# The residual's first load over two queues, and no products of ones between the rows' transpose and the residual's, in a one-core Trainium2 layer stack

## The chip, the cores and the metric

The kernel runs on one core of a Trainium2 chip. A core has a matrix engine (TensorE, PE in the profile, PEld for its weight loads), a vector engine (VectorE, DVE), an activation engine (ScalarE, ACT), GpSimd (POOL) and SyncE (SP), which here only issues transfers. Each engine works through its own instructions in order and waits on semaphores for the others. Transfers between device memory and the core's memory (SBUF, 128 partitions) are issued by SyncE or ScalarE, each on a queue of its own, and run on 16 DMA engines.

The metric is the device time of one execution in microseconds; lower is better.

## What is computed

Three layers over one sequence of 256 tokens with 1024 features, in float32: two of a first kind (a mixer, then a squared-ReLU MLP) and one of a second kind (attention and a short convolution beside each other). Cut to the frame, and to what the kernel's first microseconds compute:

```python
def rmsnorm(x, g):
    xf = x.astype(jnp.float32)
    y = xf * lax.rsqrt(jnp.mean(xf * xf, axis=-1, keepdims=True) + EPS)
    return (y * g.astype(jnp.float32)).astype(x.dtype)

for l in range(DEPTH):                       # DEPTH = 2
    g = norm_g[l]
    h = rmsnorm(x, g[0])
    y = even_mixer(h, ...) if l % 2 == 0 else odd_mixer(h, ...)
    x = x + rmsnorm(y, g[1])
    h = rmsnorm(x, g[2])
    x = x + rmsnorm(sq_relu_mlp(h, mlp_w1[l], mlp_w2[l]), g[3])
# then one hybrid layer (attention, gated convolution) and a last rmsnorm
```

The even mixer begins with `p = (h @ w_in)`; its first columns to be computed are those of `hf` (512 to 1024).

## The kernel before

**The weights come in units.** All weight matrices are cut into 1 MB units, in a fixed order (`UNITS`). SyncE loads unit after unit into a ring of four slots `raw`; ScalarE casts each to its high half `wh`, VectorE subtracts to get the low half `wl` (a *split*), and TensorE multiplies high and low halves of weights and activations: three products in place of one in float32. Of the activations, `hh` and `hl` (tile `hx` in the rows) are the high and low half. Unit 0 is loaded, cast and split in two halves.

**The start.** Nothing can be multiplied before the first normalised residual stands transposed in `hx`. The steps, in order of what feeds what:

- SyncE loads the residual `x` in two transfers of 128 tokens (128 partitions, 4 KB in each; semaphores `d_x0` and `d_x1`), then the two halves of unit 0, then units 1 and 2, then small tables.
- ScalarE first issues two transfers on its own queue: `ident`, the identity matrix for transposes (64 KB), and `rows1`, 121 rows of gains and small parameters (60.5 KB; tile `arena` in the rows); both count on `d_rows`. Then it loads a function table and takes a root of `eps`, and for each 128 tokens takes the sum of squares (waiting for `d_x0`, `d_x1`) and a root.
- VectorE (`prenorm_first`) takes the reciprocal and scales the first 128 tokens into `work_t` (semaphore `x_w`). Then it waits for `colsT`, copies the transposed rows out of their bank into `col1` (`cols`), and then does reciprocal and scaling of the second 128 tokens.
- TensorE multiplies ones by ones eight times (`idle_products(8)`, a result that nobody reads), waits for `d_rows`, transposes the rows (`colsT`), makes three more such products, and then in `x_turn_first` waits for `x_w` and transposes 2 x 8 blocks of the residual: the eight of the first tokens, then the eight of the second, signalling `x_t` after every second block of these.
- ScalarE, after the cast of unit 0's first half, waits for `x_t` and multiplies each transposed block pair by its gain into `hh`; VectorE makes `hl`; and TensorE starts unit 0 (`a_first`).

The order on each engine is the order in the code; no scheduler moves anything. The helper at L672 issues all matrix products, L1843 ScalarE's activations, L1230 to L1236 VectorE's operations. In the trace one float32 product or transpose is one or two records: the eight products of ones are 16, the 16 transposes of the residual are 16.

Of the kernel before, what the change touches and what calls it, by code (L numbers as in the profile page):

```python
# [24 lines left out]
P = 128  # L25
# [201 lines left out]
def at(role, i=0):  # L227

    return next(u for u, it in enumerate(UNITS) if it[4] == role and it[5] == i)
# [39 lines left out]
def build(nc, a, out):  # L269
    ctx = ExitStack()  # L270
    with ctx:
# [3 lines left out]
        def place(name, shape, dt, at_byte=None):  # L275
            size = int(np.prod(shape[1:])) * (1 if dt == U8 else 4)
            if at_byte is None:
                at_byte = cursor[0]
                cursor[0] += (size + 31) // 32 * 32
            return nc.alloc_sbuf_tensor_at(name, list(shape), dt, offset=at_byte)  # L280
# [4 lines left out]
        x = place("x", (P, TT, D), F32)  # L285
# [60 lines left out]
        S = {n: ctx.enter_context(nc.semaphore("s_" + n)) for n in names}  # L346
# [132 lines left out]
        def half_of(half):  # L479
            return slice(512 * half, 512 * (half + 1))  # L480
# [12 lines left out]
        def turn_count(p, j):  # L493
            return {0: 0, 2: len(TURNS[0])}[p] + j + 1
# [44 lines left out]
        def wait_low(eng, u):  # L539

            eng.wait_ge(S["lo_" + LOW_OF[u][0]], LOW_OF[u][1])

        def unit_src(u):
            kind, w, r0, c0, _, _ = UNITS[u]
            n, cols = P * SLABS[kind], UELEMS // SLABS[kind]
            return a[w][r0:r0 + n, c0:c0 + cols].rearrange("(k p) c -> p k c", p=P)
# [9 lines left out]
        def slot(t, u):  # L556
            return part(t, u).rearrange("p (k c) -> p k c", k=SLABS[UNITS[u][0]])
# [44 lines left out]

        @block.sync
        def _(eng):
            eng.dma_start(x[:, 0, :], a["x"][0:P, :]).then_inc(S["d_x0"], 16)
            eng.dma_start(x[:, 1, :], a["x"][P:2 * P, :]).then_inc(S["d_x1"], 16)
            for u in range(NU):
                if u == 3:
                    eng.dma_start(rows2[0:ROWS2, :], a["rows2"]).then_inc(S["d_small"], 16)
                    eng.dma_start(rel_in, a["rel_bias"]).then_inc(S["d_small"], 16)  # L610
                    eng.dma_start(onehot, a["tbl"][0:32, T_ONEHOT:T_ONEHOT + SEQ]).then_inc(S["d_small"], 16)
                if u == 6:
                    eng.dma_start(mask_rows, a["tbl"][:, T_MASKS:T_END]).then_inc(S["d_masks"], 16)
                if u == RING:
                    eng.dma_start(tables[:, :], a["tbl"][:, 0:T_CAUSAL]).then_inc(S["d_tables"], 16)
                if u == 8:
                    eng.dma_start(wg[:, :, :],
                                  a["od_w_in"][:, 3072:3080].rearrange("(k p) c -> p k c", p=P)).then_inc(S["d_wg"], 16)
                    eng.dma_start(gzb[:, :], a["gate_b"].broadcast_to([P, 8])).then_inc(S["d_wg"], 16)
                if u == at("mv"):  # L620

                    eng.wait_ge(S["y_ret"], 2)
                    eng.dma_start(tables[:, 0:384], a["tbl"][:, T_CAUSAL:T_CAUSAL + 384]).then_inc(S["d_causal"], 16)
                for n, (v, i) in enumerate((("up0", 3), ("up0", 8), ("up1", 3), ("up1", 8))):
                    if u == at(v, i):
                        if n % 2 == 0:
                            eng.wait_ge(S["yl_turn"], turn_count(n, len(TURNS[n]) - 1))
                        else:
                            eng.wait_ge(S["x_n"], 4 * n)
                        src = a["rows1"]  # L630
                        eng.dma_start(grow, bass.AP(tensor=src.tensor, offset=src.offset + P * (16 * n + 8),
                                                    ap=[[0, P], [1, D]])).then_inc(S["d_grow"], 16)
                if u == at("aq", 1):
                    eng.wait_ge(S["mod"], 12)
                    eng.dma_start(gate_dram.rearrange("o (k p) -> p (o k)", p=P), mod[:, 16:24],
                                  allow_slow_non_contiguous=True).then_inc(S["d_gate"], 16)
                if u == at("out5"):

                    eng.wait_ge(S["aout"], ATT_HEADS)
                    eng.wait_ge(S["d_gate"], 16)  # L640
                    eng.dma_start(fin_gate, gate_dram.broadcast_to([P, D])).then_inc(S["d_gain"], 16)
                    eng.dma_start(fin_gain, a["final_gain"].broadcast_to([P, D])).then_inc(S["d_gain"], 16)
                if u == at("av"):

                    eng.wait_ge(S["warg"], HEADS)
                    eng.wait_ge(S["gbm"], 1)
                    eng.wait_ge(S["d_u"], 16)
                    src = scratch_dram
                    eng.dma_start(bias[:, :, :], bass.AP(tensor=src.tensor, offset=src.offset,
                                                         ap=[[1, P], [384, ATT_HEADS], [1, SEQ]])).then_inc(S["d_bias"], 16)  # L650
                if u >= RING:

                    wait_low(eng, u - RING)
                if u == 0:
                    for half, landed in enumerate((S["raw_half"], raw_sem[0])):
                        c = slice(4 * half, 4 * half + 4)
                        eng.dma_start(slot(raw, 0)[:, c, :], unit_src(0)[:, c, :]).then_inc(landed, 16)
                else:
                    eng.dma_start(slot(raw, u), unit_src(u)).then_inc(raw_sem[u % RING], 16)

            for t in range(TT):
                for half, done in enumerate((S["fin_act"], S["fin_dve"])):
                    if (t, half) != (1, 0):
                        eng.wait_ge(done, t + 1)
                        eng.dma_start(out[t * P:(t + 1) * P, half_of(half)], fin_t[:, t, half_of(half)]).then_inc(S["d_out"], 16)
            eng.wait_ge(S["d_out"], 64)
# [3 lines left out]
        def _(eng):  # L670
            def mm(o, l, r, start, stop):
                return eng.matmul(o, l, r, start=start, stop=stop, skip_group_check=True)  # L672
# [267 lines left out]
            def x_turn_first():  # L940

                for t in range(TT):
                    eng.wait_ge(S["x_w"], t + 1)
                    for k in range(KT):
                        m = eng.transpose(x_bank(k)[:, t * P:(t + 1) * P], work_t[:, t, k * P:(k + 1) * P], ident[:, :])  # L945
                        if t == 1 and k % 2 == 1:
                            m.then_inc(S["x_t"], 1)

            def idle_products(n):

                for _ in range(n):
                    mm(PS[1][:, 0:SEQ], ones[:, 0:1].broadcast_to([P, P]), ones[:, 0:1].broadcast_to([P, SEQ]), True, True)
# [2 lines left out]
            idle_products(8)  # L955
            eng.wait_ge(S["d_rows"], 32)
            eng.transpose(PS[2][:, 0:ROWS1], rows1[0:ROWS1, :], ident[0:ROWS1, 0:ROWS1]).then_inc(S["colsT"], 1)
            idle_products(3)
            x_turn_first()
            eng.wait_ge(S["const"], 2)  # L960

# [879 lines left out]
        def _(eng):  # L1841
            def act(o, x, f, **more):
                return eng.activation(o, x, f, **more)  # L1843
# [13 lines left out]
            def x_root(n, t):  # L1857

                squares(junk_x[:, t, :], x[:, t, :], 4 + t, S["x_ssq"])
                eng.wait_ge(S["x_ssq"], 2 * n + t + 1)  # L1860
                root(sd[:, t:t + 1], st[:, 4 + t:5 + t], D).then_inc(S["x_sd"], 1)
# [18 lines left out]

            def prenorm_first():
                for t in range(TT):
                    eng.wait_ge((S["d_x0"], S["d_x1"])[t], 16)
                    x_root(0, t)
                high_half(0)
                eng.wait_ge(S["cols"], 1)
                for k in range(KT):
                    if k == 4:
                        high_half(1)
                    if k % 2 == 0:  # L1890
                        eng.wait_ge(S["x_t"], k // 2 + 1)
                    act(hh[:, k, :], x_bank(k), ACT.Copy, scale=col1[:, R_NORM + k:R_NORM + k + 1]).then_inc(S["hh"], 1)
                high(1)
# [74 lines left out]
            def load_roots():  # L1968

                act(sd[:, 15:16], eps[:, :], ACT.Sqrt)  # L1970

            eng.dma_start(ident[:, :], a["tbl"][:, T_IDENT:T_IDENT + P]).then_inc(S["d_rows"], 16)
            eng.dma_start(rows1[0:ROWS1, :], a["rows1"]).then_inc(S["d_rows"], 16)
            eng.wait_ge(S["const"], 2)
# [147 lines left out]
            for u in range(-AHEAD, NU):  # L2122
# [53 lines left out]
                elif role in ("rq", "rk"):  # L2176
# [4 lines left out]
                    half = P // 2  # L2181
# [110 lines left out]
```

## Time and profile before

| | |
|---|---|
| median of 3 runs | 973.98 us (973.92 to 974.48) |
| the profiled execution's own time | 974.07 us |
| its span, first to last instruction | 972.0 us |
| TensorE busy | 964.2 us (99%) |
| VectorE busy | 682.1 us (70%) |
| ScalarE busy | 539.9 us (56%) |
| TensorE's first product of unit 0 | 10.80 us after the span's start |

The shares are averages over the span. The change touches only the first eleven microseconds, so the timeline and the chain of waits of that stretch are the views to read; the share of busy time says only that TensorE has hardly a gap after them. A busy TensorE at the start includes the products of ones, which compute nothing. A row of the timeline gives start, duration, engine, line and tiles, and in brackets how long the engine sat idle before and what ended that.

### The profile page before, as it was taken

What the parts mean: (1) busy time and instruction counts of PE and PEld (TensorE: products, weight loads), DVE (VectorE), ACT (ScalarE), POOL (GpSimd) and SP (SyncE); (2) the same over time, 40 slices, a digit from 0 to 9 for tenths busy, and PEclk for the clock granted to TensorE, in tenths of its full rate; (3) what the DMA queues carried; (4) which work ended last, traced back from release to release, by engine and by line L of the source; (5) the groups of instructions that cost most, each with busy time, mean ns of one, the idle gap of its engine ahead of it and who ended that gap; (6) DMA issues with size and microseconds to landing.
All of it is one profiled execution on the core that took longest, in us unless ns stands there. A gap on an engine that the chain in (4) does not pass through costs nothing.

```text
span 972.0 us, 13041 instructions
## 1 busy us (share of the span) xinstructions
PE 964.2 (99%) x5192; PEld 832.9 (86%) x5192; DVE 682.1 (70%) x917; ACT 539.9 (56%) x733; POOL 13.9 (1%) x12
## 2 busy tenths in 40 slices
PE   9999999999999999999999999999999999999997
PEld 8898888888888888988888888887888888888886
DVE  6989646687677767866687767768554888756474
ACT  7844464664555457655674455558445576545533
POOL 0000000000000000000000000000000000002000
PEclk9999999999999999999999999999999999999999
DMA  9954526467776674534467777773855544566611
GB/s 330 302 174 130 173 89 197 130 228 265 226 242 225 231 245 135 178 130 130 152 216 256 242 225 243 247 219 117 271 194 178 170 139 165 173 215 221 207 51 43
DMA packets 122863, 187.27 MB, mean 193 GB/s; under 512 B 5331, under 2 KB 88756, under 8 KB 122804
## 3 DMA queue, kind: packets, MB, share of 16 engines
q1 hardware_dynamic: 122368, 186.05, 58.1%
q8 instruction: 41, 0.67, 0.3%
q10 hardware_dynamic: 436, 0.40, 0.1%
q14 instruction: 18, 0.15, 0.0%
HBM read 185.37 MB, written 1.06 MB: 192 GB/s over the span
## 4 chain that ended last, share of the span: by engine, by line
PE 96%; DVE 3%; ACT 1%; issue 0%; ACTq 0%
PE bank L672 94%; DVE arena L1236 1%; DVE wl L1230 1%; PE bank L936 1%; PE bank L1026 0%; ACT arena L1843 0%; DVE arena L1233 0%; DVE arena L1230 0%; PE bank L1109 0%; ACT L1843 0%; ACT wh L1848 0%; PE bank L879 0%; PE bank L735 0%; PE bank L945 0%; ACT sd L1843 0%
## 5 line engine op out<-in xcount | busy, mean ns | idle before, releaser
L1230 DVE TENSOR_TENSOR wl<-raw,wh 128x2048 fp32r<-128x2048 f32 (+1 forms) x157 | 356.7, 2275 | 152.1 <-ACT wh L1848 128.1
L1848 ACT CAST wh<-raw 128x2048 fp32r<-128x2048 f32 x155 | 294.7, 1911 | 142.7 <-PE bank L672 141.0
L672 PE MATMUL bank<-hx,wh 128*128 128x512 f32 (+1 forms) x1280 | 296.6, 364 | 0.1
L672 PEld LDWEIGHTS bank<-hx,wh 128*128 128x128 f32 x1280 | 219.4, 190 | 30.4 <-issue 0.7
L672 PE MATMUL bank<-wh,hx 128*128 128x512 f32 x576 | 184.5, 394 | 0.8 <-ACT hx L1843 0.5
L672 PE MATMUL bank<-hx,wl 128*128 128x256 f32 x1088 | 174.3, 282 | 0.0
L672 PEld LDWEIGHTS bank<-hx,wl 128*128 128x128 f32 x1088 | 156.7, 190 | 8.9
L672 PE MATMUL bank<-wh,yh 128*128 128x512 f32 (+1 forms) x420 | 163.4, 389 | 0.0
L672 PE MATMUL bank<-wl,yh 128*128 128x512 f32 (+1 forms) x420 | 162.7, 387 | 0.0
L672 PE MATMUL bank<-wh,yl 128*128 128x512 f32 (+1 forms) x420 | 162.6, 387 | 0.0
L672 PEld LDWEIGHTS bank<-wh,hx 128*128 128x128 f32 x576 | 107.8, 188 | 24.3 <-issue 2.0
L672 PE MATMUL bank<-wl,hx 128*128 128x512 f32 x288 | 112.2, 390 | 0.0
L672 PEld LDWEIGHTS bank<-wh,yl 128*128 128x128 f32 x420 | 78.9, 188 | 16.2
L672 PEld LDWEIGHTS bank<-wh,yh 128*128 128x128 f32 x420 | 78.9, 188 | 15.5
L672 PEld LDWEIGHTS bank<-wl,yh 128*128 128x128 f32 x420 | 79.0, 188 | 15.3
L1230 DVE TENSOR_TENSOR arena<-bank,arena 128x256 f32<-128x256 f32 (+1 forms) x89 | 40.7, 488 | 44.3 <-ACT arena L2195 29.5
L672 PEld LDWEIGHTS bank<-wl,hx 128*128 128x128 f32 x288 | 54.1, 188 | 10.6
L2195 ACT COPY arena<-bank 128x256 f32<-128x256 f32 x56 | 18.1, 376 | 74.1 <-PE bank L672 74.1
L1988 ACT COPY work<-bank 128x256 f32<-128x256 f32 x56 | 20.6, 368 | 52.2 <-PE bank L672 52.2
L1843 ACT ACTIVATE arena<-bank 128x512 f32<-128x512 f32 (+2 forms) x58 | 28.4, 498 | 32.9 <-PE bank L672 32.8
L1236 DVE SCALAR_TENSOR_TENSOR arena<-raw,cf,arena 128x256 f32<-128x256 f32 x84 | 40.7, 485 | 3.0
L1843 ACT ACT_TABLE_LOAD x26 | 33.4, 1283 | 4.3 <-PE bank L672 2.0
(187 smaller groups left out, 675.0 us busy)
## 6 DMA issues: line engine op xcount, KB each, us to landing
raw<-in_mlp_w SPq DMA_DIRECT2D x64, 1024.0 KB, 5.4
raw<-in_w_in SPq DMA_DIRECT2D x40, 1024.0 KB, 5.1
raw<-in_ev_w_in SPq DMA_DIRECT2D x19, 1024.0 KB, 5.5
raw<-in_w_ada SPq DMA_DIRECT2D x12, 1024.0 KB, 5.1
raw<-in_od_w_in SPq DMA_DIRECT2D x12, 1024.0 KB, 5.2
raw<-in_ev_w_out SPq DMA_DIRECT2D x6, 1024.0 KB, 4.9
raw<-in_od_w_out SPq DMA_DIRECT2D x4, 1024.0 KB, 4.8
raw<-in_w_o_conv SPq DMA_DIRECT2D x4, 1024.0 KB, 4.8
```

Of the source, the lines that this page charges most:

```text
L672: return eng.matmul(o, l, r, start=start, stop=stop, skip_group_check=True)
L936: m = eng.transpose(x_half(t, k), src[:, t, k * P:(k + 1) * P], ident[:, :])
L1230: return eng.tensor_tensor(o, x, y, op)
L1236: return eng.scalar_tensor_tensor(out=o, in0=x, scalar=c, in1=y, op0=op0, op1=op1)
L1843: return eng.activation(o, x, f, **more)
L1848: eng.copy(part(wh, u), part(raw, u)).then_inc(S["hi"], 1)
L1988: eng.copy(up_home(i)[:, g * SEQ:(g + 1) * SEQ], up_block(u, g)[1][:, SEQ:2 * SEQ]).then_inc(S["up_low"], 1)
L2195: m = eng.copy(wide_home(u, g), wide_bank(u, g)[:, SEQ:2 * SEQ])
```

## The change

Two edits. First, each transfer of `x` is cut into two of 64 partitions: SyncE issues the lower halves, ScalarE the upper ones, both counting on the semaphore of their 128 tokens, for which ScalarE's squares now wait for 32. ScalarE issues its two before `ident` and `rows1`, so that these come third and fourth in its queue. Second, `idle_products(3)` between the transpose of the rows and that of the residual is gone; the eight before stay.

```diff
         @block.sync
         def _(eng):
-            eng.dma_start(x[:, 0, :], a["x"][0:P, :]).then_inc(S["d_x0"], 16)
-            eng.dma_start(x[:, 1, :], a["x"][P:2 * P, :]).then_inc(S["d_x1"], 16)
+            half = P // 2
+            eng.dma_start(x[0:half, 0, :], a["x"][0:half, :]).then_inc(S["d_x0"], 16)
+            eng.dma_start(x[0:half, 1, :], a["x"][P:P + half, :]).then_inc(S["d_x1"], 16)
...
             eng.transpose(PS[2][:, 0:ROWS1], rows1[0:ROWS1, :], ident[0:ROWS1, 0:ROWS1]).then_inc(S["colsT"], 1)
-            idle_products(3)
             x_turn_first()
...
                 for t in range(TT):
-                    eng.wait_ge((S["d_x0"], S["d_x1"])[t], 16)
+                    eng.wait_ge((S["d_x0"], S["d_x1"])[t], 32)
                     x_root(0, t)
...
+            half = P // 2
+            eng.dma_start(x[half:P, 0, :], a["x"][half:P, :]).then_inc(S["d_x0"], 16)
+            eng.dma_start(x[half:P, 1, :], a["x"][P + half:2 * P, :]).then_inc(S["d_x1"], 16)
             eng.dma_start(ident[:, :], a["tbl"][:, T_IDENT:T_IDENT + P]).then_inc(S["d_rows"], 16)
             eng.dma_start(rows1[0:ROWS1, :], a["rows1"]).then_inc(S["d_rows"], 16)
```

TensorE's instructions at the program's start, in the kernel before (`bank` is the destination; `ones` the products of ones, `ident,arena` the rows' transpose, `ident,work` the residual's, `hx,wh` unit 0):

```order
1 L672 MATMUL bank<-ones 128x256 x8
2 L957 MATMUL bank<-ident,arena 128x121
3 L672 MATMUL bank<-ones 128x256 x3
4 L945 MATMUL bank<-ident,work 128x128 x16
5 L672 MATMUL bank<-hx,wh 128x256 x8
```

and in the changed kernel:

```order
1 L673 MATMUL bank<-ones 128x256 x8
2 L958 MATMUL bank<-ident,arena 128x121
3 L946 MATMUL bank<-ident,work 128x128 x16
4 L673 MATMUL bank<-hx,wh 128x256 x8
5 L673 MATMUL bank<-hx,wl 128x256 x8
```

The residual's transposes now stand directly behind the rows'. ScalarE's instructions at the program's start, as the difference from the kernel before (line numbers shift by one to three):

```order
-L1972 DMA ident<-in_tbl 128x128
-L1973 DMA arena<-in_rows 121x128
+L1973 DMA x<-in_x 64x1024
+L1974 DMA x<-in_x 64x1024
+L1975 DMA ident<-in_tbl 128x128
+L1976 DMA arena<-in_rows 121x128
 L1843 ACT_TABLE_LOAD
 L1843 ACTIVATE sd<-eps 128x1
```

Two transfers have come ahead of the two that were there, and ahead of the table load; VectorE's instructions are unchanged.

## Rows read from the trace of the kernel before

**Rows 1.** The page: busy time, share of the span, instructions; shares of the chain.
```profile
PE 964.2 (99%) x5192; PEld 832.9 (86%) x5192; DVE 682.1 (70%) x917; ACT 539.9 (56%) x733; POOL 13.9 (1%) x12
...
PE 96%; DVE 3%; ACT 1%; issue 0%; ACTq 0%
```

**Rows 2.** The chain in order of time, start us, us, what; 0 to 31 us.
```profile
0.92 6.65 PE bank L672 x16
...
7.68 1.31 PE bank L672 x6
8.99 1.75 PE bank L945 x16
...
10.80 17.82 PE bank L672 x144
```

**Rows 3.** The timeline, 0 to 30 us: start us, us, engine, line; idle before.
```profile
0.74 0.42 ACTq L1972 DMA_DIRECT2D ident<-in_tbl  x1
...
1.19 0.63 ACTq L1973 DMA_DIRECT2D arena<-in_rows  x1
...
1.86 1.28 ACT L1843 ACT_TABLE_LOAD   x1 [1.86 <-issue]
...
4.87 1.06 ACT L1843 ACTIVATE arena<-x 128x1024 f32<-128x1024 f32 x1 [1.52 <-DMA x<-in_x]
...
6.26 1.04 ACT L1843 ACTIVATE arena<-x 128x1024 f32<-128x1024 f32 x1
...
6.66 0.75 DVE L1233 TENSOR_SCALAR work<-x,rs 128x1024 f32<-128x1024 f32 x1
...
7.42 0.29 ACT L1843 ACTIVATE sd<-st,eps 128x1 f32<-128x1 f32 x1
...
7.72 0.28 DVE L1281 COPY col<-bank 128x121 f32<-128x121 f32 x1 [0.31 <-PE bank L957]
...
8.11 0.75 DVE L1233 TENSOR_SCALAR work<-x,rs 128x1024 f32<-128x1024 f32 x1
8.41 1.05 ACT L1879 CAST wh<-raw 128x1024 fp32r<-128x1024 f32 x1 [0.70 <-DMA raw<-in_ev_w_in]
...
8.83 1.91 PE L945 MATMUL bank<-ident,work 128*128 128x128 f32 x16
9.56 1.22 DVE L1230 TENSOR_TENSOR wl<-raw,wh 128x1024 fp32r<-128x1024 f32 x1 [0.70 <-ACT wh L1879]
...
10.19 1.57 ACT L1843 ACTIVATE hx<-bank,col 128x256 fp32r<-128x256 f32 x4 [0.72 <-PE bank L945]
...
11.06 1.66 DVE L1236 SCALAR_TENSOR_TENSOR hx<-bank,col,hx 128x256 fp32r<-128x256 f32 x4 [0.27 <-ACT hx L1843]
...
16.12 4.48 DVE L1230 TENSOR_TENSOR wl<-raw,wh 128x2048 fp32r<-128x2048 f32 x2
...
22.70 0.40 PE L672 MATMUL bank<-hx,wh 128*128 128x256 f32 x2
```

**Rows 4.** Windows: us, busy us by engine (x), PEclk, DMA busy share, GB/s.
```profile
1.00:2.00 1.00, 1.00 (x3) 0.82 (x4) 0.31 (x1) 0.14 (x1) 0.00 (x0) 1.00 0.36 61
2.00:3.00 1.00, 1.00 (x4) 0.81 (x3) 0.00 (x0) 1.00 (x1) 0.00 (x0) 1.00 0.63 200
3.00:4.00 1.00, 1.00 (x3) 0.79 (x3) 0.00 (x0) 0.34 (x2) 0.00 (x0) 1.00 1.00 366
4.00:5.00 1.00, 1.00 (x4) 0.74 (x3) 0.00 (x0) 0.13 (x1) 0.00 (x0) 1.00 1.06 417
```

**Rows 5.** The tile x, 0 to 12 us, SyncE's two loads.
```profile
DMA to landing us min/median/max: 4.1/4.6/5.0
```

**Rows 6.** Products of ones, by form: 0.9 to 6.9 us, then 6.9 to 8.6.
```profile
L672 PE MATMUL bank<-ones 128*128 128x256 f32 x14 | 6.2, 634 | 0.9 <-DVE eps L1353 0.9
...
L672 PE MATMUL bank<-ones 128*128 128x256 f32 x8 | 2.1, 396 | 0.0
```

**Rows 7.** TensorE's longest wait behind the start: us in total, times, longest us.
```profile
PE bank L672 <- ACT hx L1843: 0.5, 1, 0.5
```

## The prediction, made before the changed kernel ran

> **What bounds the kernel now.** Begin with the page: TensorE is busy for 99% of the span, and the chain that ended last is 96% TensorE [rows 1]. Moving the start of the first real product moves the end, unless a later stage waits for something that doesn't move along. The list of TensorE's waits has little in it; the longest after the start is 0.5 us [rows 7]. So two questions remain: what holds the first product at 10.80, and does anything behind it catch up.
>
> Read next the chain in order of time [rows 2]. It runs through TensorE alone: the eight products of ones (0.92 to 7.57, in the trace two matmuls each, hence x16), the three (7.68 to 8.99, x6), the sixteen transposes of the residual (8.99 to 10.74), then `hx`. TensorE looks full and does no useful work up to 7.4. Beside it, in the timeline [rows 3]: `x` lands and ScalarE starts its squares at 4.87 and 6.26; VectorE scales the first 128 tokens by 7.41 (6.66 + 0.75), but TensorE takes up their transposes only at 8.83, since it works in order and stands in the three products. The second 128 tokens are scaled at 8.11 to 8.86. ScalarE is ready for `hx` at 9.46 (the cast at 8.41, 1.05 long, which waited for the first half of weight unit 0) and sits until 10.19.
>
> **Part 1, the three products go.** In the row of the chain they are 1.31 us. Not all of it comes back, for the second tokens are late next. Step by step. (1) The eight products end at 7.57 and the transpose of the rows at about 7.68, as before. (2) The first tokens' eight transposes follow at once: sixteen take 1.91 us [rows 3], 0.12 each, so 0.9 for eight: 7.7 to 8.6. (3) The second tokens' scaling doesn't move: VectorE first copies `col1` out of the bank at 7.72, as soon as the rows are transposed, and only then takes reciprocal and scaling; it ends at 8.86. TensorE waits about 0.3 us for it. (4) From the first transpose at 8.83 to ScalarE's first `hx` at 10.19 are 1.36 us, 0.9 of them the first tokens'; so 0.5 from the second tokens' first transpose to `hx`. A weight load and a semaphore lie before it; I take 0.25 (between nothing and 0.3, the idle VectorE shows before its copy [rows 3]). 8.86 + 0.25 + 0.5 = 9.61. (5) ScalarE is free at 9.46, 0.15 earlier. The first `hx` moves from 10.19 to 9.61, **0.58 us**, and at most 0.7 (to the cast's end); the first product from 10.80 to 10.22.
>
> Does it stay? Within unit 0 the pace is set by ScalarE's four `hx` in 1.57 us, which move whole. VectorE's split ends at 10.78 (9.56 + 1.22), and its low halves, begun at 11.06, can begin at about 10.85. TensorE needs the first of them after 16 products, about 12.5; all four are done then (10.85 + 1.66). Units 1 and 2 hang on transfers that don't move, and have slack: unit 2's split is done at 20.60 (16.12 + 4.48) and TensorE begins it at 22.70, so at 22.1 in future [rows 3]. I take 0.57 of the 0.58 as kept, and none to 0.7 as the bounds.
>
> **Part 2, `x` over two queues.** ScalarE's sequencer gets two more issues. Its two now take 0.42 and 0.63 us, and the table load follows at 1.86 [rows 3]; it goes to 2.7 to 3.1 and, with 1.28 for itself and a small root behind it, is over by 4.2 to 4.6. The first `x` lands at about 4.84 (issued at 0.74, the shorter landing 4.1 [rows 5]). Nothing in the sum, 0.25 us spare at the worst.
>
> How soon does `x` land? The engines are busy 0.36 and 0.63 in the second and third microsecond and full after that [rows 4]. A second queue could fill at most 0.64 + 0.37 = 1.0 us; then it would land up to 1 us earlier; at the other end, no sooner than now. Also `ident` and the rows (64 + 60.5 KB) no longer go beside `x` but behind it: 0.127 MB at 366 to 417 GB/s, 0.3 us for `x`. I take 0.3 earlier. In the sum it is **nothing**: the first tokens' transposes can't start before 7.7 though they are scaled at 7.41, and the second tokens' scaling waits for the rows' transpose, not for their root (done at 7.71 now, 7.42 + 0.29, while the copy runs to 8.00). The cover is the eight products; were they gone too, these 0.3 us would count.
> The Trainium skill (DMA: Bandwidth & Descriptors, Rules for kernel authors) says of two transfers to disjoint halves of the partitions "Don't bother": from two issuing engines they interleave on the same 16 engines. By it `x` lands as before, by the busy shares it may land sooner; the sum is 973.5 by either, but the rule leaves this half of the change nothing to pay for its risk, which is the next term.
>
> **What moves behind `x`.** `ident` and `rows1` are needed for every transpose at the start. They were first in ScalarE's queue, and the page shows no landing for them, only that TensorE had them by 7.4. Bound it by bytes [rows 4]: 61 + 200 + 366 + 417 = 1044 KB are moved by 5.0, which is all of `x` (1049). Then come 249 rows of 512 bytes, 127 KB. Alone: 0.35 us. Turn about with SyncE's weight rows of 1 KB: 127 + 255 KB at 350 GB/s, 1.1 us. Behind all of weight unit 0 (1049 KB more): 3.4 us. From last byte to semaphore I take 0.8 us: 627 KB are moved by 4.0, `x`'s first 524 among them, and it lands at 4.84. So 6.2, 6.9 or 9.2. I take **6.9**, as `ident` and `rows1` share turns with `x` in the same way now. TensorE asks for them at 7.4, so there is 0.5 us of slack. Past that each 0.1 us costs 0.1, through VectorE's copy and scaling to `hx`.
> The first half of weight unit 0 has the same bytes ahead of it as before, so its cast stays at 8.41; bounds 0.4 either way (the 0.127 MB of `ident` and the rows at 350 GB/s, ahead or behind). A delay of more than 0.15 is paid in full, for ScalarE does that cast before `hx`. I take 0.
>
> **Sum.** The profiled execution took 974.07 us, 2.1 more than its span of 972.0, and stands 0.1 over the median 973.98. 974.07 - 0.57 = **973.5**.
>
> **Rivals.**
> A. The rows come late. If `d_rows` completes at 8.0 (7.4 + 0.6), the gain is gone: 974.1. At the late bound, 9.2, the first product is 1.2 us later than now: 975.3. For it: they stand behind 524 KB in a queue that has only half the turns. Against: that queue ends its share of `x` when SyncE's does, and `ident` and `rows1` need only 16 turns per engine.
> B. The weights' half or another gate takes the place of the wait: the cast ends at 10.0 rather than 9.46, and the change is nil, 974.0. For it: 0.15 us of slack is little. Against: the same bytes stand ahead.
> C. The other side: the clock. TensorE starts at its lower level: 14 halves of a product take 5.98 us up to 6.9 (0.43 each, 634 ns on the row), and the next 8 read 396 ns on average and stand twice as close, six in 1.31 us of the chain [rows 2, 6]; 1.2 GHz, then 2.4, though the granted clock of the windows reads 1.00 throughout [rows 4]. The three products kept the engine full from there to the transposes. Without them it has some 0.3 us of nothing before the second tokens' transposes and about 0.4 before `hx`, and, in case A, up to 1.6 more. If it falls back to 1.2 GHz in the start and stays there as long as it did at first (6 us), 3 us of work are lost: 973.5 + 3 = 976.5. It decides only if the level falls at all. Against: engine work on both sides of each gap, which are short beside the 6 us.
> The Trainium skill (TensorE: Matmul & The Clock Gate, HAM oscillation) tells of a kernel whose products stop for a transfer each time and start slow again; by that rule case C would come with A.
> D. The change does less than it says, as the pace of the eight products varies between executions: where the level rises sooner they end sooner, and `hx` comes soon after the cast's end at 9.46 in the kernel before. Then the gain is about 0.1 to 0.2: 973.8. The three runs of before lie between 973.92 and 974.48, so something of half a microsecond does vary.
>
> **How the numbers follow.** Forecast 0.53 (973.2 to 973.8); A 0.17, spread over 973.6 to 975.3, most below 974.7; B 0.08; C 0.05; D 0.15. A measurement of this kernel can tell about 0.2%, 1.95 us, from no change. Faster than 972.0 has no mechanism that I see, the largest gain at the start being 0.7: 0.02 for the unseen. Slower than 975.9 is C: 0.05. Same 0.93. The range, 972.9 to 974.9, holds the forecast, D, B, nearly all of A, and the half microsecond by which runs differ.
>
> **What would show it.** Right: `hx` begins at 9.5 to 9.7, first product near 10.2; the rows' transpose stays at 7.4 to 7.7; TensorE's idle of about 0.3 us sits before the second tokens' transposes; VectorE's second scaling is still at 8.1; ScalarE's first square starts at 4.4 to 4.8; the span from the first product to the end stays 961.2. Wrong: the rows' transpose past 7.6 with TensorE waiting for a DMA (A); the cast of the first half later than 8.5 (B); transposes or first `hx` products at twice their spacing (C); the eight products done well before 7.57 (D); or waits behind 10.8 that weren't there.

## The result, and the profile of the changed kernel

The changed kernel is slower: 977.63 us median of 6 runs (976.7 to 978.58) against 974.22 for the kernel before in the same session (973.91 to 974.5); ratio 1.0036, 95% interval 1.0027 to 1.0046. Forecast were 973.5 and a range of 972.9 to 974.9. The six executions lie in two groups of three, 976.7 to 976.9 and 978.3 to 978.6, with the median between them; the profile is one of the longer ones. The profiled execution took 978.32 us with a span of 976.3, against 974.07 and 972.0.

The page's row of busy times, to be held against [rows 1]: by its share TensorE looks as it did, which is why the start has to be read by itself.

```profile
PE 965.6 (99%) x5186; PEld 834.6 (85%) x5186; DVE 682.1 (70%) x917; ACT 540.4 (55%) x733; POOL 13.9 (1%) x12
```

The chain in order of time, 0 to 31 us (start us, us, what). In [rows 2] it ran through TensorE from 0.92 on; now it runs through ScalarE's sequencer, which issues the two halves of `x` and `ident` until 2.84, and then through a transfer:

```profile
2.88 7.27 DMA arena<-in_rows
...
10.19 0.46 PE bank L958
10.66 3.41 PE bank L946 x16
14.07 16.97 PE bank L673 x135
```

`rows1` (tile `arena`) were issued at 2.88 and had landed at 10.15. The timeline (start us, us, engine, line, tiles; idle before), to be read against [rows 3]:

```profile
1.36 0.84 ACTq L1974 DMA_DIRECT2D x<-in_x  x1
...
3.53 1.28 ACT L1843 ACT_TABLE_LOAD   x1 [3.53 <-issue]
...
5.31 1.06 ACT L1843 ACTIVATE arena<-x 128x1024 f32<-128x1024 f32 x1 [0.29 <-DMA x<-in_x]
...
7.93 1.06 ACT L1843 ACTIVATE arena<-x 128x1024 f32<-128x1024 f32 x1 [1.15 <-DMA x<-in_x]
...
9.81 1.04 ACT L1879 CAST wh<-raw 128x1024 fp32r<-128x1024 f32 x1 [0.40 <-DMA raw<-in_ev_w_in]
...
10.19 0.46 PE L958 MATMUL bank<-ident,arena 121*128 121x121 f32 x1 [3.31 <-DMA arena<-in_rows]
...
10.45 3.62 PE L946 MATMUL bank<-ident,work 128*128 128x128 f32 x16
...
11.08 0.75 DVE L1233 TENSOR_SCALAR work<-x,rs 128x1024 f32<-128x1024 f32 x1
...
12.89 1.57 ACT L1843 ACTIVATE hx<-bank,col 128x256 fp32r<-128x256 f32 x4 [2.04 <-PE bank L946]
...
13.72 2.05 PE L673 MATMUL bank<-hx,wh 128*128 128x256 f32 x8
...
16.59 2.08 PE L673 MATMUL bank<-hx,wh 128*128 128x256 f32 x16
```

The squares start at 5.31 and 7.93 instead of 4.87 and 6.26, so `x` itself came later, not sooner; TensorE stands still for 3.31 us until the rows are there; then its 16 transposes take 3.62 us instead of 1.91; and the first product starts at 13.72 instead of 10.80. Between the last two rows and their counterparts in the kernel before it falls back further. TensorE in the kernel before, the same two groups:

```profile
10.80 1.51 PE L672 MATMUL bank<-hx,wh 128*128 128x256 f32 x8
...
13.10 2.08 PE L672 MATMUL bank<-hx,wh 128*128 128x256 f32 x16
```

13.72 is 2.92 later than 10.80; 16.59 is 3.49 later than 13.10. Why shows in TensorE's windows of the changed kernel (us, busy us (x instructions), PEclk, DMA share, GB/s):

```profile
7.00:9.00 2.00, 0.00 (x0) 0.98 1.11 309
9.00:10.00 1.00, 0.00 (x0) 0.50 1.09 331
...
12.00:14.00 2.00, 2.00 (x11) 0.50 1.10 348
14.00:16.00 2.00, 2.00 (x13) 0.57 1.10 348
16.00:18.00 2.00, 2.00 (x19) 1.00 1.13 303
...
421.90:425.30 3.40, 3.40 (x9) 0.50 0.47 193
```

The engine did nothing from 6.89 to 10.19, and from about 9 until shortly before 16 us its granted clock was half, 1.2 GHz. It fell once more in mid-kernel, between 421.9 and 425.3, and that is the last of the loss: the same products on `arena` start at 412.99 before and 416.46 now, 3.47 later, and behind the dip the same products of `wh` with `hx` at 424.44 and 428.70, 4.26 later. The whole span is 4.3 longer.

How the transfers ran between 2 and 7 us (us, PEclk, DMA busy share, GB/s), before and then changed:

```profile
2.00:7.00 5.00, 1.00 0.95 339
```

```profile
2.00:7.00 5.00, 1.00 1.00 235
```

The 16 DMA engines are as busy, and move almost a third less.

### The profile page after: what moved, and what is told of

Read it like the earlier page. It is cut to its first block, busy times and chain, and to the rows that moved or that the text cites. A ratio compares the mean times of both kernels' runs of the same rounds, so it can differ in the third digit from the quotient of the medians.

```text
span 976.3 us, 13031 instructions
## 1 busy us (share of the span) xinstructions
PE 965.6 (99%) x5186; PEld 834.6 (85%) x5186; DVE 682.1 (70%) x917; ACT 540.4 (55%) x733; POOL 13.9 (1%) x12
## 4 chain that ended last, share of the span: by engine, by line
PE 98%; DMA 1%; ACT 0%; ACTq 0%; issue 0%; DVE 0%
PE bank L673 96%; DMA arena<-in_rows 1%; PE bank L937 1%; PE bank L1026 0%; PE bank L946 0%; PE bank L1109 0%; PE bank L880 0%; PE bank L736 0%; ACT arena L1843 0%; ACTq L1974 0%; ACTq L1975 0%; ACT sd L1843 0%; ACTq L1973 0%; PE bank L958 0%; DVE x L1230 0%
```

## The experiments

Ten kernels, two of them timed twice, each beside the kernel before, whose median was 974.17 to 974.27. A time is the median of 4 to 11 executions, and there is one profile for each timing.

**The products alone.** The kernel before without `idle_products(3)`:

```diff
-            idle_products(3)
```

> The kernel before, with the three products between the transposes taken out and x loaded as before. Theory 1 (the loss comes from the transfers: the identity and the rows land late, and TensorE, idle for them, falls to its lower clock): the products alone cost nothing to remove; the rows are there by 7.4 us, the first product starts near 10.2 instead of 10.8 us, time 973.4 to 973.9, 0.2 to 0.6 below the kernel before, granted clock as before. Theory 2 (the products held the clock, and without them it falls whatever the transfers do): the transposes stand 0.2 us apart instead of 0.12, granted clock 0.994 to 0.998, time 976 to 978.

Measured: 974.33 us median, ratio 1.0000 (0.9991 to 1.0009). The clock holds, so theory 2 is out. But theory 1's gain isn't there either, though in the profile the start did gain all of it:

```profile
8.09 0.76 DVE L1232 TENSOR_SCALAR work<-x,rs 128x1024 f32<-128x1024 f32 x1
...
8.90 1.10 PE L945 MATMUL bank<-ident,work 128*128 128x128 f32 x8 [0.34 <-DVE work L1232]
...
9.44 1.57 ACT L1842 ACTIVATE hx<-bank,col 128x256 fp32r<-128x256 f32 x4 [0.51 <-PE bank L945]
...
10.06 1.51 PE L672 MATMUL bank<-hx,wh 128*128 128x256 f32 x8
```

The first product is 0.74 us earlier than 10.80. TensorE's waits between 20 and 60 us (us in total, times, longest), of which the kernel before has none in that stretch:

```profile
PE bank L672 <- ACT arena L1842: 0.7, 1, 0.7
```

And ScalarE in front of it, on weight unit 4:

```profile
25.27 1.90 ACT L1847 CAST wh<-raw 128x2048 fp32r<-128x2048 f32 x1 [2.54 <-DMA raw<-in_ev_w_in]
```

In the kernel before ScalarE waited 1.29 us there and cast at 24.62. Unit 4 landed no sooner for the earlier start, rather 0.6 later, and behind its cast ScalarE has the table loads, two more casts and the copies out of the banks that TensorE wants back near 37 us. The span ends up 0.3 longer than before (972.3 and 972.0). Why unit 4 came later than before, and not just as late, no run shows.

**Is it unit 4?** The same kernel with the 896 KB of tables loaded behind unit 4:

```diff
-                if u == RING:
+                if u == RING + 1:
                     eng.dma_start(tables[:, :], a["tbl"][:, 0:T_CAUSAL]).then_inc(S["d_tables"], 16)
```

> The kernel before without the three products, and with the 896 KB of tables loaded behind weight unit 4 instead of ahead of it. Removing the products alone started TensorE 0.74 us sooner and the end did not move: TensorE then waited 0.7 us for ScalarE near 37 us, and ScalarE had been waiting for unit 4, which landed at 25.25. If that landing is what took the gain: unit 4 lands near 22.5, TensorE does not wait there, and the time is 973.1 to 973.6, 0.7 to 1.1 below the kernel before. If the gain goes elsewhere: 974.0 to 974.5 as without the move.

Measured: 973.47 us, ratio 0.9993 (0.9984 to 1.0002). ScalarE casts units 3 and 4 without a gap:

```profile
21.15 3.71 ACT L1847 CAST wh<-raw 128x2048 fp32r<-128x2048 f32 x2
```

TensorE has no wait between 20 and 60 us. The first product starts at 10.36, 0.44 earlier than before, and the span is 0.5 shorter, so here the gain of the start is kept. Timed again with the kernel without the move beside it:

> The same kernel as e9_unit4_first, timed again beside the other two for a narrower answer: no products between the transposes, tables behind unit 4. If unit 4's landing took the gain: 973.1 to 973.7, 0.5 to 1.0 below the kernel without the table's move; if not, level with it.

> The same kernel as e1_no_products, timed again in the same session as the one with the tables moved: 974.0 to 974.6, level with the kernel before, because TensorE waits again near 37 us.

Measured: 973.34 with the move (ratio 0.9995, 0.9986 to 1.0004), 974.79 without (1.0003, 0.9995 to 1.0012). The wait is gone and both medians are 0.7 to 0.8 below the kernel before, as expected; 974.79 is 0.2 above what was expected, and the distance between the two, 1.45, is more than the 0.5 to 1.0. That unit 4's landing took the gain is shown by the traces and by the move; as a ratio to the kernel before, each interval still holds "no change". The 22 runs of this kernel fall into two groups, 14 from 973.2 to 973.51 and 8 from 973.95 to 974.16. Its two profiles are one of each. The execution of 973.5 us, then that of 974.04: first product, and TensorE's windows in mid-kernel (us, busy, PEclk, DMA share, GB/s):

```profile
10.36 1.50 PE L672 MATMUL bank<-hx,wh 128*128 128x256 f32 x8
...
417.30:420.70 3.40, 3.40 (x17) 1.00 0.67 275
```

```profile
10.03 1.51 PE L672 MATMUL bank<-hx,wh 128*128 128x256 f32 x8
...
417.30:420.70 3.40, 3.40 (x11) 0.51 0.59 239
```

The second starts 0.3 earlier and its span is 0.5 longer (972.0 and 971.5). So the dip is worth some 0.8 us, and it comes and goes in one and the same kernel. What brings it on stays open. In the kernel before the chain runs through VectorE there (409.9 to 419.9) and then ScalarE (to 424.3), but the list of TensorE's waits has only one in that stretch, 0.3 us for ScalarE.

**The transfers alone.** The changed kernel with the three products put back:

```diff
+            idle_products(3)
             x_turn_first()
```

> The changed kernel with the three products put back; only the transfers differ from the kernel before. Theory 1 (late rows, then the lower clock): the rows are transposed near 10.2 us as in the changed kernel, the clock falls in the idle stretch before, and the three products stand at the lower clock on the path: 978.5 to 981, worse than the changed kernel. Theory 2 (the products' removal is the loss): the clock holds, 974 to 975.

Measured: 979.35 us, ratio 1.0049 (1.0035 to 1.0062), theory 1 by the time and the late rows. TensorE's waits, the whole kernel:

```profile
PE bank L958 <- DMA arena<-in_rows: 3.8, 1, 3.8
```

The transfers alone make the whole loss. The products' removal doesn't add to it, rather takes some off: the medians are 1.7 apart (979.35 and 977.63), though the intervals of the two ratios overlap, and in the trace the three stand behind the late rows, on the path (10.43 to 12.18). One thing didn't come as expected: in the profiled execution, at 978.21 the shortest of four, TensorE has nothing to do from 6.48 to 10.27 and its granted clock still reads 1.00 up to 11 us; it is 0.50 only from 12 to 14. Both profiles show the lower clock after such an idle stretch, but not at the same distance from it.

**Lateness and clock apart.** The changed kernel, with TensorE kept busy until the rows are nearly there:

```diff
-            idle_products(8)
+            idle_products(15)
```

> The changed kernel with 15 products of ones ahead of the rows' transpose instead of 8, so that TensorE is busy until about 10 us. Rows and x land as in the changed kernel. If the lower clock behind the idle stretch is a cost of its own: no fall, transposes 0.12 us apart, first product near 13.0 us, time 975.9 to 976.5, about 1 to 2 us below the changed kernel. If only the lateness of the rows costs: first product near 13.7 as now and 977 to 978.5.

Measured: 976.40 us, ratio 1.0021 (1.0012 to 1.0030), 1.2 below the changed kernel.

```profile
0.92 8.97 PE L673 MATMUL bank<-ones 128*128 128x256 f32 x30 [0.92 <-DVE eps L1353]
...
10.17 0.32 PE L958 MATMUL bank<-ident,arena 121*128 121x121 f32 x1 [0.27 <-DMA arena<-in_rows]
...
10.33 1.04 PE L946 MATMUL bank<-ident,work 128*128 128x128 f32 x8
...
12.88 1.51 PE L673 MATMUL bank<-hx,wh 128*128 128x256 f32 x8
```

The rows are as late (10.17), the clock stays up, the first eight transposes take 1.04 us, and the first product starts at 12.88. So of the 2.92 us at the start 2.08 are lateness and 0.84 the clock, by one profile of each kernel.

**The rows' place in the queue.** The changed kernel with `ident` and `rows1` issued ahead of ScalarE's halves of `x`:

```diff
+            eng.dma_start(ident[:, :], a["tbl"][:, T_IDENT:T_IDENT + P]).then_inc(S["d_rows"], 16)
+            eng.dma_start(rows1[0:ROWS1, :], a["rows1"]).then_inc(S["d_rows"], 16)
             eng.dma_start(x[half:P, 0, :], a["x"][half:P, :]).then_inc(S["d_x0"], 16)
             eng.dma_start(x[half:P, 1, :], a["x"][P + half:2 * P, :]).then_inc(S["d_x1"], 16)
-            eng.dma_start(ident[:, :], a["tbl"][:, T_IDENT:T_IDENT + P]).then_inc(S["d_rows"], 16)
-            eng.dma_start(rows1[0:ROWS1, :], a["rows1"]).then_inc(S["d_rows"], 16)
```

> The changed kernel with the identity and the rows issued ahead of ScalarE's halves of x. Theory 1a (the place behind x is all that makes the rows late, and x itself is served well by two queues): rows transposed by 7.6 us, x lands as in the kernel before, 973.5 to 974. Theory 1b (the loads of 64 partitions are slow in themselves, about 1.2 us for each 256 KB in the trace of the changed kernel, one behind the other): rows early, but the second tokens' squares start at 8 us or later, first product near 12, 975 to 976.5; the clock depends on whether TensorE's idle time before the second tokens is long.

Measured: 979.23 us, ratio 1.0051 (1.0036 to 1.0066), worse than either expected, though the rows were transposed at 7.03. ScalarE's first and second squares:

```profile
8.30 1.06 ACT L1843 ACTIVATE arena<-x 128x1024 f32<-128x1024 f32 x1 [3.71 <-DMA x<-in_x]
...
10.83 1.06 ACT L1843 ACTIVATE arena<-x 128x1024 f32<-128x1024 f32 x1 [1.05 <-DMA x<-in_x]
```

Now the upper halves are the late ones. The squares are 3.4 and 4.6 us later than in the kernel before, and the clock fell here too. What stands behind in ScalarE's queue comes late, and the order only picks which that is.

**Width or queue?** All four halves on SyncE's queue:

```diff
         @block.sync
...
             eng.dma_start(x[0:half, 0, :], a["x"][0:half, :]).then_inc(S["d_x0"], 16)
+            eng.dma_start(x[half:P, 0, :], a["x"][half:P, :]).then_inc(S["d_x0"], 16)
             eng.dma_start(x[0:half, 1, :], a["x"][P:P + half, :]).then_inc(S["d_x1"], 16)
+            eng.dma_start(x[half:P, 1, :], a["x"][P + half:2 * P, :]).then_inc(S["d_x1"], 16)
...
         @block.scalar
...
-            eng.dma_start(x[half:P, 0, :], a["x"][half:P, :]).then_inc(S["d_x0"], 16)
-            eng.dma_start(x[half:P, 1, :], a["x"][P + half:2 * P, :]).then_inc(S["d_x1"], 16)
```

> The changed kernel with all four transfers of x of 64 partitions on SyncE's queue; ScalarE issues the identity and the rows first, as in the kernel before. Theory S (a transfer to 64 partitions moves slower, whatever its queue; in the changed kernel each of 256 KB took about 1.2 us with the engines shown busy): x lands at 5.2 to 5.8 and 7.4 to 8.0 us, the rows by 6.5, first product at 11.3 to 12, time 975 to 976. Theory Q (the two queues take turns and hold each other up; the width is harmless): x lands as in the kernel before, 4.9 and 6.2, 974 to 974.5.

Measured: 976.80 us, ratio 1.0024 (1.0014 to 1.0033). With no `x` on ScalarE's queue the rate between 2 and 7 us is as low as in the changed kernel:

```profile
2.00:7.00 5.00, 1.00 1.01 231
```

The squares start at 6.21 and 8.63, later than expected, and the clock fell here too. Theory S. The other way round, two queues but full width, each bringing half of the columns to all 128 partitions:

```diff
-            eng.dma_start(x[0:half, 0, :], a["x"][0:half, :]).then_inc(S["d_x0"], 16)
+            eng.dma_start(x[:, 0, 0:D // 2], a["x"][0:P, 0:D // 2]).then_inc(S["d_x0"], 16)
...
-            eng.dma_start(x[half:P, 0, :], a["x"][half:P, :]).then_inc(S["d_x0"], 16)
+            eng.dma_start(x[:, 0, D // 2:D], a["x"][0:P, D // 2:D]).then_inc(S["d_x0"], 16)
```

> The changed kernel with x split by columns instead of partitions: each queue brings 512 of the 1024 columns to all 128 partitions, in the same order ahead of the identity and the rows. Theory S: x lands near 5.0 and 6.3 us, the rows at 7 to 8.5, first product at 10.2 to 11.5, time 974.2 to 975.2. Theory Q: as the changed kernel, x at 5.3 and 7.9, rows at 10.1, 976.7 to 978.6.

Measured: 974.43 us, ratio 1.0003 (0.9994 to 1.0012), theory S.

```profile
2.00:7.00 5.00, 1.00 1.00 330
```

```profile
4.55 1.06 ACT L1842 ACTIVATE arena<-x 128x1024 f32<-128x1024 f32 x1 [0.20 <-DMA x<-in_x]
...
6.02 1.06 ACT L1842 ACTIVATE arena<-x 128x1024 f32<-128x1024 f32 x1
...
8.30 0.32 PE L957 MATMUL bank<-ident,arena 121*128 121x121 f32 x1 [0.84 <-DMA arena<-in_rows]
...
11.02 1.50 PE L672 MATMUL bank<-hx,wh 128*128 128x256 f32 x8
```

`x` is there at 4.55, 0.3 us sooner than before, as the prediction had it; the rows come at 8.30, 0.8 late for TensorE, and the first product starts at 11.02. At full width two queues don't slow `x`, but the rows' place behind it still costs what the products' removal gives.

**Sixty-four rows, or sixty-four neighbouring partitions?** The changed kernel with every second partition on each queue:

```diff
-            eng.dma_start(x[0:half, 0, :], a["x"][0:half, :]).then_inc(S["d_x0"], 16)
+            eng.dma_start(x[0:P:2, 0, :], a["x"][0:P:2, :]).then_inc(S["d_x0"], 16)
...
-            eng.dma_start(x[half:P, 0, :], a["x"][half:P, :]).then_inc(S["d_x0"], 16)
+            eng.dma_start(x[1:P:2, 0, :], a["x"][1:P:2, :]).then_inc(S["d_x0"], 16)
```

> The changed kernel with its four transfers of x of 64 partitions each, but every second partition (0, 2, 4, ... on SyncE's queue; 1, 3, 5, ... on ScalarE's) in place of the lower and upper 64. Same number of rows, bytes, queues and order. Theory P (64 neighbouring partitions can be written at only some 230 GB/s, since they reach only half of the way into SBUF): every second one reaches all of it, the engines move 320 to 350 GB/s between 2 and 7 us, x lands near 4.6 and 6.1 us, the rows near 8.3, 974.2 to 975.2 as with the columns. Theory N (64 rows per transfer are slow by their number, as each engine gets only four): 230 to 250 GB/s, x at 5.3 and 7.9, rows at 10.1, 976.5 to 978.6 as the changed kernel.

Measured: 975.78 us, ratio 1.0017 (1.0008 to 1.0026), between the two. The profile is of the shortest of the eleven executions (974.84); they go up to 976.75, six of them with a mean granted clock of 0.996 or 0.997 where the profiled one has 0.998, and what else differs in those no profile shows. Its windows:

```profile
1.00:2.00 1.00, 1.00 0.00 0
2.00:3.00 1.00, 1.00 0.65 131
3.00:4.00 1.00, 1.00 0.77 242
4.00:5.00 1.00, 1.00 1.05 393
5.00:6.00 1.00, 1.00 0.99 370
...
2.00:7.00 5.00, 1.00 0.91 302
```

Once running, the engines move 370 to 393 GB/s, as theory P says, where the changed kernel moves 254 and 205 between 4 and 6; the second squares start at 6.60 and TensorE gets the rows at 8.99. So neighbouring partitions are what keeps the rate at 204 to 262. But nothing is moved before 2 us, and the issues are long (0.56 and 0.58 on SyncE, 0.57 and 0.86 on ScalarE), as in the changed kernel and unlike the full width (0.39 to 0.45): sixty-four rows per transfer have a price of their own, in the issue, in either shape. From 2 to 4 us this kernel is even slower than the changed one (131 and 242 GB/s against 250 and 262), which is why its mean from 2 to 7 is 302 and not the 320 to 350 of theory P; why, stays open.

The chains of the three kernels part the two prices. The transfer of the rows, from its issue to its landing (start us, us, what), with `x` by columns and then with every second partition; in the changed kernel it was 2.88 and 7.27:

```profile
2.15 6.10 DMA arena<-in_rows
```

```profile
2.89 6.06 DMA arena<-in_rows
```

So the rows come at 8.25, 8.95 and 10.15: 0.7 for the long issues ahead of theirs, and 1.2 for the neighbouring partitions.

The Trainium skill (SBUF — State Buffer, Door 1: The DMA port swizzle, and "Can I just issue two DMAs to hit both halves?") says that partitions 0 to 63 reach 8 of the 16 ports and 64 to 127 the other 8, and that two transfers don't combine to reach all of them. The 235 and 231 GB/s, and the 370 to 393 with every second partition, agree; the ports themselves no trace shows. It also calls one transfer over all 128 partitions the only way to reach all ports; two transfers to every second partition moved as much between 4 and 6 us as full width did, so there the measurement decides.

**Two attempts to have both.** The second 128 tokens whole on ScalarE's queue, behind the rows (and without the three products):

```diff
         @block.sync
...
-            eng.dma_start(x[:, 1, :], a["x"][P:2 * P, :]).then_inc(S["d_x1"], 16)
...
         @block.scalar
...
             eng.dma_start(rows1[0:ROWS1, :], a["rows1"]).then_inc(S["d_rows"], 16)
+            eng.dma_start(x[:, 1, :], a["x"][P:2 * P, :]).then_inc(S["d_x1"], 16)
```

> The kernel before without the three products, and with the second 128 tokens of x (all 128 partitions, one transfer) on ScalarE's queue behind the identity and the rows; the first stay on SyncE's. Theory S: x lands at 4.9 and 6.2 to 6.8 us, rows by 6.5, 974.0 to 974.6. Theory Q: the second tokens land at 7.5 us or later, 975 or more.

Measured: 976.96 us, ratio 1.0025 (1.0014 to 1.0035). Theory S failed here: the width is full, and the second tokens still come late, with the squares at 5.15 and 8.69, and the clock fell too (0.50 from 11 to 12 us).

```profile
8.69 1.06 ACT L1841 ACTIVATE arena<-x 128x1024 f32<-128x1024 f32 x1 [2.07 <-DMA x<-in_x]
```

They stand behind `ident` and the rows, 249 small rows, while SyncE's queue goes on with the weights; that the two queues take turns row by row is my reading, not shown. Then the tables' move (in the expectation "e9", the kernel of "Is it unit 4?") with `x` by columns, `ident` on SyncE's and the rows on ScalarE's queue behind the first tokens:

```diff
         @block.sync
...
+            eng.dma_start(x[:, 0, 0:D // 2], a["x"][0:P, 0:D // 2]).then_inc(S["d_x0"], 16)
+            eng.dma_start(ident[:, :], a["tbl"][:, T_IDENT:T_IDENT + P]).then_inc(S["d_rows"], 16)
+            eng.dma_start(x[:, 1, 0:D // 2], a["x"][P:2 * P, 0:D // 2]).then_inc(S["d_x1"], 16)
...
         @block.scalar
...
+            eng.dma_start(x[:, 0, D // 2:D], a["x"][0:P, D // 2:D]).then_inc(S["d_x0"], 16)
             eng.dma_start(rows1[0:ROWS1, :], a["rows1"]).then_inc(S["d_rows"], 16)
+            eng.dma_start(x[:, 1, D // 2:D], a["x"][P:2 * P, D // 2:D]).then_inc(S["d_x1"], 16)
```

> e9 with x over both queues by columns (128 partitions each), and with the identity on SyncE's queue and the rows on ScalarE's behind each queue's half of the first tokens, ahead of the second tokens. Theory S (width and the place of the rows are what hurt, not the second queue): x lands by 4.8 and 6.3 us, the rows by 6.5, first product at 9.8 to 10.3, time 972.9 to 973.5, level with e9 or up to 0.4 better. If a second queue hurts in itself: rows after 7.5 or x after 7, 974 or more.

Measured: 974.24 us, ratio 1.0005 (0.9996 to 1.0014); the first product starts at 10.97, as the second tokens' squares wait until 7.30. Expected were 9.8 to 10.3. Against `x` by columns with the rows last, the rows are transposed at 7.45 and not 8.30, and the second squares start at 7.30 and not 6.02; the first product comes at much the same time (10.97 and 11.02). The lowest medians stay those of the kernel that leaves `x` alone and moves the tables, 973.34 and 973.47.

## Why the prediction was wrong

**The step that failed is how soon the transfers land: `x` first, and the rows behind it.** For `x` the prediction set "no sooner than now" as the bad end. That bound came from rows in which every transfer of `x` was 128 partitions wide, and was taken over to transfers of 64, which no row of the kernel before shows. `x` came 0.4 us later for the first tokens and 1.7 for the second. The rule of the Trainium skill that I weighed there (DMA: Bandwidth & Descriptors, Rules for kernel authors), "Don't bother", was read as "no gain"; the runs show a loss.

**The rows were forecast at 6.9 and landed at 10.15**, outside even the late bound of 9.2. Of the 3.25 us, 1.2 are the neighbouring partitions: the sum took 1044 KB as moved by 5.0 us, from rates of 366 to 417 GB/s, and between 2 and 7 us they were 235 on average. Another 0.7 are the long issues ahead of the rows'. The remaining 1.35 has nothing to do with the width: with `x` by columns the rate was 330 and the rows still landed at 8.25, so the reckoning by bytes and turns was too early by itself, which is rival A's mechanism, with A's price. The break-even at 8.0 and "each 0.1 us costs 0.1" were right: 10.15 is 2.15 behind 8.0, and with the clock held the first product is 2.08 late.

**Rival C was the right mechanism at the wrong chance.** Its condition was a longer idle stretch by rival A, and that is what happened: 3.3 us of nothing, and half the clock. I put A at 0.17 and C at 0.05. By the Trainium skill (TensorE: Matmul & The Clock Gate, HAM oscillation) I had C come with A: at the 3.31 us measured here it did. With the stretch that I gave A, up to 1.6 us more, it might not have, for the kernel with every second partition waits 1.4 us for the rows and its profile shows no fall. C's price, at most 3 us, was 0.84 before the first product and 0.57 in unit 0.

**The sum as it was.** 2.08 us late rows + 0.84 + 0.57 slow clock at the start + 0.8 for the dip near 422 = 4.3, the difference of the spans. The dip was in no term of the prediction, and it is no effect of the change alone, since it also comes and goes without it. Three executions of the changed kernel, at 976.7 to 976.9, lie some 1.6 lower than the other three; their mean granted clock was 0.997 or 0.998 rather than 0.994, so they have less of the last three terms. Which of them they lack no profile shows.

**The products' removal.** The start moved as forecast, and 0.16 more (10.06, where the sum had 10.22): the second tokens' transposes start at 8.90, 0.05 behind the end of their scaling at 8.85, where the sum had allowed 0.25. The weights' half came sooner too (cast at 7.87, not 8.41), which left ScalarE free. "I take 0.57 of the 0.58 as kept" was wrong: in that profile nothing was kept. I had looked at units 1 and 2 and stopped; a later transfer, unit 4, was already what ScalarE waited 1.29 us for.

**Rivals B and D** had little part. The weights' half came later than forecast (cast at 9.81, not 8.41), but the rows were later still. The eight products do vary, ending at 6.89 here and at 7.57 before; in this kernel that only made the idle stretch longer.

**Right by luck**: the issues on ScalarE. "Nothing in the sum, 0.25 us spare at the worst" had them over by 4.6. They took 0.58, 0.84, 0.60 and 0.62 us, the table load moved to 3.53, not 3.1, and the small root behind it ended at 5.02, later than the 4.84 at which `x` was expected; it cost nothing there only because `x` came at 5.3. And the issues do stand on the path, as the chain shows: that of the rows begins at 2.88 instead of 1.19.

**Right were** the eight transposes at 0.12 each, and that the second scaling waits for the rows' transpose (11.08, behind the copy at 10.69).

## What to carry to other kernels

Don't split a transfer by halves of the partitions: here each half was slower and two queues didn't bring it back, while a split by columns over all partitions brought `x` 0.3 us sooner, though no faster kernel. Before more is put ahead in a queue, find the smallest and most urgent thing that will stand behind it; here 124 KB held everything. When a start is made earlier, look at every later wait for a transfer, not only the next one: a transfer that doesn't come sooner takes the gain back.

## What the runs showed of the hardware

- With loads into 64 neighbouring partitions the 16 DMA engines moved 225 to 238 GB/s between 2 and 7 us, in the five kernels that have them, at a busy share of 0.99 to 1.02; with 128 partitions 329 to 339 in the kernel before, in that without the three products and in that with `x` by columns, at 0.95 to 1.00. With every second partition it was 302, and 370 to 393 from 4 to 6. A busy share doesn't show it.
- Issuing a piece of `x` for 64 partitions took 0.55 to 0.86 us, for 128 partitions 0.36 to 0.45.
- TensorE's clock fell to 1.2 GHz in the changed kernel, where the engine had nothing to do from 6.89 to 10.19, and held in the profiled execution of the kernel with every second partition, where it waited 1.4 us for the rows. In the kernel with the transfers alone it fell between 11 and 12 us, after the idle stretch (6.48 to 10.27) and not in it. In mid-kernel it falls in some executions of one kernel and not in others, for some 0.8 us.
